# Routed experts in seven steps instead of eight, with a table of places by rank

## The reference

```python
scores = sigmoid(t @ router_w); biased = scores + router_bias
# of 4 groups of 4 experts the one with the best two is chosen, in it the two best experts
y = zeros_like(t)
for e in range(16):
    a = silu(t @ w1[e]) * (t @ w3[e])          # w1, w3: 1024 x 512
    y = y + gates[:, e:e + 1] * (a @ w2[e])    # w2: 512 x 1024
```

## Time and profile before

| | |
|---|---|
| median of 3 runs | 1209.88 us (1203.99 to 1212.16) |
| the profiled execution | 1202.03 us |
| its span, first to last instruction | 1200.2 us |
| TensorE busy | 1124.0 us, 94% |
| expert weights | 96 loads of 2 MB on SP's queue |
| longest wait of TensorE on one of these in layer 0 or 1 | 2.3 us |

### The profile page before, as it was taken

The page is one execution under the profiler, slowest core; times in us unless marked ns, Lnnn a source line. Parts: engine busy times, 40 slices in busy tenths (PEclk is TensorE's granted clock), DMA queues, the critical chain, the costliest instruction groups (busy, mean ns, idle before and its releaser), DMA issues.

```text
span 1200.2 us, 18288 instructions
## 1 busy us (share of the span) xinstructions
PE 1124.0 (94%) x8019; PEld 613.4 (51%) x8019; DVE 464.4 (39%) x996; ACT 163.8 (14%) x322; POOL 14.1 (1%) x29
## 2 busy tenths in 40 slices
PE   5899999999997999999969999999999799999994
PEld 2478767754444344434447785775444434443441
DVE  4446587541115222222246478740102512222223
ACT  2011100310023000000011110022001300000001
POOL 3000000000000000000000000000000000000000
PEclk9999999999998999999989999999999899999998
DMA  9977735538533999999994666442444299999991
GB/s 318 391 259 285 271 142 211 194 123 302 223 140 112 423 420 421 420 420 420 415 379 170 216 245 220 169 151 105 148 170 172 79 408 422 421 420 421 422 413 64
DMA packets 88868, 333.78 MB, mean 278 GB/s; under 512 B 3162, under 2 KB 3447, under 8 KB 80465
## 3 DMA queue, kind: packets, MB, share of 16 engines
q1 hardware_dynamic: 86077, 323.02, 69.2%
q0 software_dynamic: 1680, 6.26, 1.4%
q10 hardware_dynamic: 1028, 3.28, 0.8%
HBM read 331.50 MB, written 1.05 MB: 277 GB/s over the span
## 4 chain that ended last, share of the span: by engine, by line
PE 73%; DMA 21%; DVE 3%; ACT 1%; issue 1%; SPq 0%; DVEq 0%; ACTq 0%
PE bank L584 71%; DMA ring<-in_moe_w_dram 21%; PE bank L847 1%; PE bank L751 0%; SPq L534 0%; PE bank L631 0%; PE bank L928 0%; PE bank L1000 0%; ACT L1227 0%; DVE area L1331 0%; ACT xn L1290 0%; ACT xn L1110 0%; PE bank L918 0%; DMA stat<-in_hf_freq_dram 0%; DVE area L1414 0%
## 5 line engine op out<-in xcount | busy, mean ns | idle before, releaser
L584 PE MATMUL bank<-ring,hT 128*32 128x512 f32 (+3 forms) x2624 | 381.2, 567 | 14.0 <-DMA ring<-in_moe_w_dram 13.9
L584 PEld LDWEIGHTS bank<-ring,hT 128*32 128x32 f32 (+2 forms) x2624 | 154.7, 128 | 221.7 <-issue 216.6
L584 PE MATMUL bank<-hT,ring 128*32 128x256 f32 (+1 forms) x2112 | 214.0, 381 | 1.6 <-DVE hT L1372 1.6
L584 PEld LDWEIGHTS bank<-hT,ring 128*32 128x32 f32 (+1 forms) x2112 | 157.0, 132 | 58.6 <-issue 12.2
L584 PE MATMUL bank<-ring,area 128*32 128x512 f32 x1024 | 113.2, 594 | 0.9 <-ACT area L1247 0.9
L1781 DVE TENSOR_TENSOR area<-bank,area 128x512 f32<-128x512 f32 x16 | 11.1, 692 | 196.4 <-PE bank L584 196.4
L584 PE MATMUL bank<-area 32*64 32x64 f32 (+4 forms) x576 | 81.9, 334 | 0.0
L584 PEld LDWEIGHTS bank<-area 32*64 32x64 f32 (+3 forms) x576 | 41.4, 151 | 52.3 <-issue 51.0
L584 PEld LDWEIGHTS bank<-ring,area 128*32 128x32 f32 x1024 | 31.7, 110 | 70.1 <-issue 67.0
L584 PE MATMUL bank<-area,xn 128*128 128x128 f32 x512 | 62.7, 283 | 0.1
L584 PEld LDWEIGHTS bank<-area,xn 128*128 128x128 f32 x512 | 61.1, 199 | 0.3
(11 more groups left out here) (241 smaller groups left out, 775.4 us busy)
## 6 DMA issues: line engine op xcount, KB each, us to landing
ring<-in_moe_w_dram SPq DMA_DIRECT2D x96, 2048.0 KB, 16.7
ring<-in_w_in_dram SPq DMA_DIRECT2D x26, 2048.0 KB, 10.6
ring<-in_w_ada_dram SPq DMA_DIRECT2D x24, 2048.0 KB, 9.0
ring<-in_w_out_dram SPq DMA_DIRECT2D x4, 2048.0 KB, 8.0
ring<-in_w_br_h_dram SPq DMA_DIRECT2D x4, 1536.0 KB, 7.0
ring<-in_w_br_a_dram SPq DMA_DIRECT2D x2, 1024.0 KB, 5.1
area<-in_decay_dram POOLq DMA_DIRECT2D x2, 768.0 KB, 11.2
cst<-in_cst_dram POOLq DMA_DIRECT2D x1, 1464.0 KB, 9.0
```

The costliest lines, as they stand in the source:

```text
L584: return pe.matmul(dst, lhsT, rhs, start=start, stop=stop, skip_group_check=True)
```

## The change

The experts are worked in seven steps. Step 0 is as it was. Step 1 takes four experts, the ranks 8 to 11, with 32 columns each; steps 2 and 3 take ranks 0 and 13, and 1 and 12, with 96 and 32 columns; steps 4 to 6 take ranks 2 to 7 in pairs of 64 columns. First column and capacity of a rank come from a constant table instead of arithmetic on the rank. `order_i` gets its own semaphore event, ahead of this arithmetic, and the flag `over` a new one. The ring still has six buffers; step 1 has twelve blocks.

```diff
-CAP_HEAVY = 96
-CAP_LIGHT = P - CAP_HEAVY
+PLAN = (((8, 1), (9, 1), (10, 1), (11, 1)), ((0, 3), (13, 1)), ((1, 3), (12, 1)),
+        ((2, 2), (3, 2)), ((4, 2), (5, 2)), ((6, 2), (7, 2)))
+STEPS = 1 + len(PLAN)
+RANKS = [()] + [tuple(r for r, _ in step) for step in PLAN]
+TILES = [(0, 0, 1, 1)] + [tuple(e for e, (_, n) in enumerate(step) for _ in range(n)) for step in PLAN]
+MOE = [(s, m, e) for s in range(STEPS) for m in range(3) for e in range(max(TILES[s]) + 1)]
...
-                                                        for r in (s - 1, RANKED - s)]
+                                                        for r in RANKS[s]]
...
-                            ws[j >= split][:, k, :], k == 0, k == ND - 1)
+                            ws[TILES[s][j]][:, k, :], k == 0, k == ND - 1)
...
-                dv.tensor_copy(order_i[:, :], small[0])
-
-                dv.tensor_scalar(small[1], rank, -1.0, float(RANKED), ALU.mult, ALU.add)
...
+                dv.tensor_copy(order_i[:, :], small[0]).then_inc(v_order, 1)
+
+                link(dv.tensor_tensor(square, inner(rank), outer(iota[:, 0:NE]), ALU.is_equal))
+                dv.tensor_tensor(placed, square, outer(rank_base), ALU.mult)
+                link(dv.tensor_tensor(fitted, square, outer(rank_cap), ALU.mult))
+                dv.tensor_reduce(base, placed, AX.X, ALU.add)
+                link(dv.tensor_reduce(capc, fitted, AX.X, ALU.add))
```

More of the change, by code:

```diff
@@ L61 @@
 TAPS_C = 1
-BPP = 6
 RING = 6
@@ L141, in constants @@
     tab[:, C_STEP:C_STEP + STEPS] = P * np.arange(STEPS) + 1
-    tab[:, C_SORTED:C_SORTED + NE] = 1.0
     tab[:, C_BASE:C_BASE + NE] = 1.0
     for j, e in enumerate(FIRST):
-        tab[:, C_SORTED + e] = 0.0
-        tab[:, C_BASE + e] = 1 + j * CAP_FIRST - CAP_HEAVY
-        tab[:, C_CAP + e] = CAP_FIRST - CAP_LIGHT
+        tab[:, C_BASE + e] = 1 + j * CAP_FIRST
+        tab[:, C_CAP + e] = CAP_FIRST
+    for s, step in enumerate(PLAN):
+        col = (s + 1) * P
+        for r, n in step:
+            tab[:, C_RBASE + r] = col
+            tab[:, C_RCAP + r] = 32 * n
+            col += 32 * n
     tab[:, C_UP:C_UP + EPG * EPG] = np.triu(np.ones((EPG, EPG)), 1).reshape(1, -1)
@@ L277, in trunk_kernel @@
         small = [region(NE) for _ in range(3)]
-        square = region(NE * NE).rearrange("p (a b) -> p a b", a=NE)
+        square, placed, fitted = [region(NE * NE).rearrange("p (a b) -> p a b", a=NE) for _ in range(3)]
         four = region(4 * NT * NE).rearrange("p (j t e) -> p j t e", j=4, t=NT)
@@ L447, in trunk_kernel @@
         blocks = [(L,) + key for L in range(DEPTH)
-                  for key in (*head(L), *(("moe", n) for n in range(STEPS * BPP)))]
+                  for key in (*head(L), *(("moe", key) for key in MOE))]
         place = {key: n for n, key in enumerate(blocks)}
@@ L472, in released @@
                 return p_wo, L * 4 + 2 * b + 2
-            s, j = b // BPP, b % BPP
-            return (p_up, (L * STEPS + s) * 2 + 1 + j // 2) if j < 4 else (p_down, (L * STEPS + s + 1) * 2)
+            s, m, _ = b
+            return (p_up, (L * STEPS + s) * 2 + 1 + m) if m < 2 else (p_down, (L * STEPS + s + 1) * 2)
         def acc(L, n):
@@ L983, in up @@
                     n = L * STEPS + s
-                    split = 2 if s == 0 else 3
-                    ws = [landed("moe", s * BPP + 2 * which + e)[:, :].rearrange("p (k f) -> p k f", f=FE) for e in range(2)]
+                    ws = [landed("moe", (s, which, e))[:, :].rearrange("p (k f) -> p k f", f=FE) for e in range(max(TILES[s]) + 1)]
                     for k in range(ND):
@@ L1007, in down @@
                     n = L * STEPS + s
-                    split = 2 if s == 0 else 3
                     pe.wait_ge(a_actT, n + 1)
-                    ws = [landed("moe", s * BPP + 4 + e)[:, :].rearrange("p (k f) -> p k f", f=D) for e in range(2)]
+                    ws = [landed("moe", (s, 2, e))[:, :].rearrange("p (k f) -> p k f", f=D) for e in range(max(TILES[s]) + 1)]
                     for h in range(2):
@@ L1045, in _ @@
                 scatter(STEPS - 1)
-                pe.wait_ge(v_order, L + 1)
+                pe.wait_ge(v_over, L + 1)
                 settle(pe)
```

44 lines of the change are left out of this document (19 added, 25 removed).

## The result

The changed kernel takes **1226.38 us** (median of 4 runs, 1222.68 to 1231.46) against 1209.72 (1203.99 to 1212.16) for the kernel before, timed beside it: 1.0139 times, 95% interval 1.0089 to 1.0189. The two profiled executions lie 20.7 us apart (spans 1220.9 and 1200.2).

What follows compares the result with a forecast made beforehand. SP's queue of expert weights was taken as the bound. Per layer 1.2 + 1.2 + 2.15 - 0.5 = 4.05 us, 8.1 for two layers, on the 1209.88 median gave 1218.0 us ("same"), range 1208 to 1229.

Steps and rivals of the forecast that it cites:

- The bound: Expert parts: SP's queue sets the pace at 5.03 us a block; removing 28.8 us of TensorE work a layer saves nothing.
- Table and registers: Before step 1's first issue: 1.2 us for the table on VectorE plus 1.2 us for two more register loads, a layer.
- The hand-overs: Step 1's two up bursts and down(1), twelve blocks through six buffers: queue gaps of 2.15 us a layer, bounds 0 and 5.4.
- the budget: Data still queued when step 1's four blocks have landed: two blocks, 10.06 us, less some 0.3 for the landing signal, 9.8.
- the refill: Time from an issue after a step 1 burst until data flow: 1.0 us to first bytes, 2.0 us to a steady stream.
- No gap, at the full clock: Step 1 hand-overs with warm bursts: 8.2 to 9.2 us against 9.8 us of queued data, so the queue never runs dry.
- I am wrong if the queue shows holes of several us: The prediction's own sign of failure in the profile after; the other was a mean block time leaving 5.03 us.
- The clock: Step 1 bursts starting cold take 1.4 to 2.4 us longer; gaps put at 0.85 per up and 0.45 for down(1).
- rival 1: All step 1 bursts cold, refill 2.0 us, three gaps of 1.8 us: 8.2 us a layer, 1226; 0.27 with half-way cases.
- The return: Transfers gain from fewer TensorE bursts reading the buffers: at most 1.5 us a layer, taken as 0.5.
- Rival 2: No queue gaps at step 1's hand-overs: 1212 to 1215 us; shares 0.68 for "same" with the sum, which has two thirds.
- rivals 3 and 4: 3: over 1% faster, transfers speeding up where TensorE rests (0.04); 4: expert outgrows its columns, at least 480 us (0.01).

Runs made afterwards that it cites:

- seven_pairs: The changed kernel with step 1 worked two experts at a time, each half releasing its own two blocks: 1212.05 us, 1.0015 of the kernel before.
- seven_buf7: The changed kernel with a seventh 2 MB buffer in an idle area of the mixing part: 1200.95 us, 0.9919 of the kernel before.
- seven_warm: The changed kernel with 6, 12 and 4 unused matmuls on constants ahead of step 1's three bursts: 1221.39 us, 1.0095 of the kernel before.

## Why the prediction was right in its range and wrong in its forecast

- **The bound** held. SP's queue of expert weights sets the pace; blocks take 5.02 us (120.55 / 24) where they flow. 28.8 us a layer less work on TensorE moved nothing, and its waits rose to 69.5 us, as forecast (about 70).
- **Table and registers**: forecast 2.4 us a layer, measured 2.25 and 2.36 to the first issue. In layer 0 both halves stand as forecast: a stop of 1.03 us within `up(0, 0)`, ended by `rows_to_h`, and 1.1 us between the burst's end and the issue (2.67 against 1.59 before). In layer 1 the `gather` ran longer at the lower clock (6.45 us against 5.16) and no stop was left. There the table was hidden, and the 2.36 us are 1.1 of registers and 1.3 of clock: that it meets the forecast of 2.4 too is luck. The timeline of layer 0:

```profile
379.18 1.36 DVE L1759 TENSOR_SCALAR hT<-bank,A,modT 128x128 f32<-128x128 f32 x4
380.60 10.51 PE L590 MATMUL bank<-ring,hT 128*32 128x512 f32 x96 [1.03 <-DVE hT L1759]
384.30 0.60 ACT L1249 ACTIVATE area<-bank 128x512 f32<-128x512 f32 x1 [7.25 <-PE bank L590]
386.97 0.36 SPq L540 DMA_DIRECT2D ring<-in_moe_w_dram  x1
```

- **The hand-overs** are the step that failed: forecast 2.15 us a layer, measured 6.5 and 8.4. The mechanism, the three places and TensorE's waits (7.0, 13.3 and 5.4 us; forecast 6, 13 and 4) were right. Wrong was first the budget: "9.8 (10.06 less some 0.3 for the landing signal)" should have been 8.1 to 9.3, 8.5 in the mean, because the signal waits for the last of sixteen engines. Then the refill: reckoned from the blocks that followed, data flowed at full rate 1.9 to 2.1 us behind the issue at all six places, the upper end of the forecast's 1.0 to 2.0. "No gap, at the full clock" therefore had no margin: 7.1 for the burst, 0.2 to its start, and 2.0 for the refill are 9.3 us against 8.5. Last the price of the clock: it was taken as 1.4 to 2.4 us for the `up` and at half for `down(1)`, and measured 1.5 to 2.9, at every burst. These three are larger than forecast by about 1.3, 0.5 and 0.5 to 1.2 us a place. For the mean engine they make holes of 8.2 and 9.7 us a layer; what TensorE waits for, the signals, lost less, since their lag shrank in the holes (from 1.7 to 1.1 us in layer 0). The 0.6 us to the first byte, for which the prediction names the Trainium skill and which it sets against its rows, fits them when counted from the end of the issue: at 419.60 the issue began, at 419.93 it ended, and the first transfer started at 420.57. It is the 2 us to the full rate that keep the gaps open. By the prediction's own sign ("I am wrong if the queue shows holes of several us") its account of the hand-over was wrong in size.
- **The clock**: the `up` bursts were cold, at 9.1 and 9.9 us in layer 0 and 8.9 and 10.0 in layer 1, so 1.8 to 2.9 us over a warm one. `down(1)`, put at half, was cold too, 8.6 and 9.9 us; that is rival 1's reading. The Trainium skill, "TensorE: Matmul & The Clock Gate", section "HAM oscillation — how this bites in real kernels", which the prediction cites for bursts shorter than the waits between them, points the right way: all six bursts of step 1 started cold, after 5.4 to 13.3 us of idle time. But only the second wait of a layer (13.3 and 12.7 us) was longer than its burst; the other four started cold too. In the prediction's reading of the earlier trace rows the clock falls at 367.6; the row's 0.77 puts it at 367.8, which changes nothing.
- **The return**: forecast 0.5 us, measured none. Behind the first issue the holes read from the bursts sum to 6.3 and 8.7, the whole surplus is 6.5 and 8.4, so blocks went no faster in between than the mean of 5.03 us. (By the 4.89 and 5.11 us of step 1's own blocks the holes are 7.2 and 9.7; then 0.7 and 1.3 us came back elsewhere, from what is open.)
- **The rivals.** Rival 1 is what happened, in place and nearly in size: its 8.2 us a layer against 8.7 and 10.8. That its 1226 us meets 1226.38 is luck: it had holes of 1.8 us each, and they were 1.1 to 3.9; its issue terms were too high by 0.5; and the median moved less than the profile (16.7 us against 20.7). The range held because this rival's price was its upper end. The point from which it decides, 1.2 us a gap, was passed at five of six. Rival 2 fell with the microsecond at 419 in which nothing starts; rivals 3 and 4 show nowhere.

The ratio's interval begins at 0.9% slower, so "slower by over 1%" is likely and not certain. The sum of the parts, 19.5 us in the profile, and `seven_pairs` at 1.0015 and `seven_buf7` at 0.9919 say that the loss is real and where it is. Open is how it divides between the clock and the depth, which only the estimates above tell.

## What to carry to other kernels

When a step needs more blocks than the ring holds, add up one hand-over: burst at the **lower** clock, issue, and 2 us of refill, against the data still queued **less the lag of the landing signal** (0.8 to 1.8 us here); where that doesn't hold, release blocks in smaller groups or find one more buffer. Read the lag off windows: from the landing signal to the microsecond in which a queue with known bytes runs dry. A saving on an engine that only keeps pace with a queue is worth nothing, and it can cost something if its new grain starves that queue.

## What the runs showed that was not expected

- The landing signal of a 2 MB block lay 0.8 to 1.8 us behind the mean end of its data, because the sixteen DMA engines did not end together: at the fourth block of step 1 one of them trailed the next by 0.75 us, and the signal came 0.45 us behind it.
- The length of a wait does not say alone whether a burst runs cold. In `seven_warm` the clock fell for bursts that followed 2.08, 2.56 and 2.88 us of idle time (the first two behind 10.6 us of dense matmuls), and not for those after 1.69, 1.96 and 3.18. It fell when the burst had already begun, 0.1 us after its start at 432.34 and 1.1 us after that at 1015.01. In `seven_pairs` bursts after 2.60 and 2.85 us were warm and one after 2.79 was cold.
- An area that is idle for part of the kernel is worth 6 us a layer as a seventh buffer, mostly because one block goes out 7 us before the first release.
- Where TensorE is at its lower clock at the head of the expert part differs between executions and moves a part by 1 to 2 us and the stretches between by up to 6. Profiles of two kernels are compared from one landmark to the next, not end to end.
